# Feed-forward groups 1 and 2: a tile's gate and up products as seven block products in place of eight

## What is computed

```python
def swiglu(x, w_gate, w_up, w_down):
    return (jax.nn.silu(x @ w_gate) * (x @ w_up)) @ w_down

f1 = swiglu(rmsnorm(x, ffn1_pre_g), ffn1_w_gate, ffn1_w_up, ffn1_w_down)
x = x + 0.5 * rmsnorm(f1, ffn1_post_g)
...                                   # the mixer
f2 = swiglu(rmsnorm(x, ffn2_pre_g), ffn2_w_gate, ffn2_w_up, ffn2_w_down)
x = x + 0.5 * rmsnorm(f2, ffn2_post_g)
```

## Time and profile before

| what | value |
|---|---|
| time, three runs | median 1166.08 us (1164.78 to 1174.18) |
| profiled execution, span from first to last instruction | 1167.8 us |
| TensorE busy (matmul) | 1120.6 us, 9522 matmuls |
| VectorE busy | 615.3 us |
| ScalarE busy | 329.2 us |
| GpSimd busy | 42.9 us |
| mean granted TensorE clock | 0.964 |
| DMA | 91.99 MB, mean 79 GB/s |

### The profile page before, as it was taken

The page is one execution under the profiler, slowest core; times in us unless marked ns, Lnnn a source line. Parts: engine busy times, 40 slices in busy tenths (PEclk is TensorE's granted clock), DMA queues, the critical chain, the costliest instruction groups (busy, mean ns, idle before and its releaser), DMA issues. The chain is left out here.

```text
span 1167.8 us, 22671 instructions
## 1 busy us (share of the span) xinstructions
PE 1120.6 (96%) x9522; PEld 1097.9 (94%) x9522; DVE 615.3 (53%) x1015; ACT 329.2 (28%) x496; POOL 42.9 (4%) x57
## 2 busy tenths in 40 slices
PE   6999999999999999999899989999999999999996
PEld 6999999999999999999777789999999999999996
DVE  5534344323434778788869637873434333243446
ACT  5321222112222334331234433442122221122221
POOL 0000000000000000030223000000000000000001
PEclk9999999999999979999779989899999999999998
DMA  6322323222232221232601002213232322222222
GB/s 216 95 80 90 108 72 103 78 90 91 72 108 72 73 86 38 63 88 60 96 2 39 2 1 93 73 41 95 77 113 72 108 72 90 90 82 98 72 73 77
DMA packets 35394, 91.99 MB, mean 79 GB/s; under 512 B 10368, under 2 KB 12928, under 8 KB 35328
## 3 DMA queue, kind: packets, MB, share of 16 engines
q1 hardware_dynamic: 34320, 88.78, 25.0%
q10 hardware_dynamic: 1008, 2.27, 0.6%
HBM read 87.76 MB, written 3.28 MB: 78 GB/s over the span
## 5 line engine op out<-in xcount | busy, mean ns | idle before, releaser
L306 PE MATMUL ps<-xh,wh 128*128 128x272 f32 x1840 | 404.0, 293 | 16.4 <-DVE xl L503 8.6
L306 PE MATMUL ps<-xh,wl 128*128 128x272 f32 x1840 | 400.3, 291 | 0.0
L306 PE MATMUL ps<-xl,wh 128*128 128x272 f32 x1840 | 399.3, 290 | 0.0
L306 PEld LDWEIGHTS ps<-xh,wh 128*128 128x128 f32 x1840 | 299.3, 191 | 19.0 <-DVE wl L289 9.0
L306 PEld LDWEIGHTS ps<-xl,wh 128*128 128x128 f32 x1840 | 299.6, 191 | 0.0
L306 PEld LDWEIGHTS ps<-xh,wl 128*128 128x128 f32 x1840 | 297.7, 191 | 0.0
L284 ACT ACTIVATE wh<-raw 128x1024 fp32r<-128x1024 f32 (+1 forms) x163 | 168.1, 1034 | 324.6 <-PE ps L306 208.6
L289 DVE TENSOR_TENSOR wl<-raw,wh 128x1024 fp32r<-128x1024 f32 (+1 forms) x163 | 192.8, 1203 | 38.0 <-ACT wh L284 37.7
L306 PE MATMUL ps<-hh,wh 128*128 128x272 f32 x704 | 157.7, 290 | 0.0
L306 PE MATMUL ps<-hh,wl 128*128 128x272 f32 x704 | 156.7, 290 | 0.0
L306 PE MATMUL ps<-hl,wh 128*128 128x272 f32 x704 | 156.5, 289 | 0.0
(11 more groups left out here) (312 smaller groups left out, 790.3 us busy)
## 6 DMA issues: line engine op xcount, KB each, us to landing
raw<-in_w_gu SPq DMA_DIRECT2D x88, 512.0 KB, 3.6
raw<-in_w_d SPq DMA_DIRECT2D x32, 512.0 KB, 3.6
raw<-in_w_in SPq DMA_DIRECT2D x19, 512.0 KB, 3.6
raw<-in_w_d SPq DMA_DIRECT2D x16, 384.0 KB, 3.0
raw<-in_w_out SPq DMA_DIRECT2D x8, 512.0 KB, 3.6
out_y<-x SPq DMA_DIRECT2D x16, 136.0 KB, 1.7
x<-in_x ACTq DMA_DIRECT2D x4, 272.0 KB, 5.6
x<-in_x SPq DMA_DIRECT2D x4, 272.0 KB, 6.7
```

The source lines that it names most:

```text
L306: last = pe.matmul(out[:, n], left[:, s, j], right[:, j, n * H:n * H + H], start=first and opens and j == order[0], stop=final and closes ...
```

## The change

Groups 1 and 2 of both blocks (32 of the 44 hidden tiles) compute gate and up together. The two weight tiles, each halved along the 1024 rows, make a 2 x 2 block matrix (row blocks gate and up, column blocks the halves); the activations, halved along the rows and along the tokens, make another. The 2 x 2 block product, eight block products in the kernel before, is done with seven (Strassen's scheme in Winograd's form), each of 4 x 3 = 12 matmuls: 84 a tile where there were 96.

- **Sums of weights.** Four of the seven left factors are not blocks of the weights but sums of them. GpSimd makes them, four additions of 128 x 512 a tile (`fast_pool`), in columns of `xh` and `xl` that the seven products don't read. All seven factors are then split as before, by five ScalarE copies (`fast_hi`) and five VectorE subtractions (`fast_lo`) a tile, three of 512 and two of 1024 columns, where there were two and two of 1024. The seven factors have one buffer each.
- **Sums of activations.** Four right factors are sums too. They are made once for each feed-forward block, while TensorE does the down units of group 0, in four rounds: ScalarE scales two rows (`rows_act`), GpSimd adds (`ffn_pool`), ScalarE and VectorE split (`rows_hi_act`, `rows_lo_dve`).
- **Recombination.** A tile uses four PSUM banks, alternately 0 to 3 and 4 to 7. The products 0, 2, 4, 6 pile up in one bank, and ScalarE copies what lies there after 0, 2 and 4 (`fast_copy`), so TensorE waits for a copy ahead of the products 2, 4, 5 and 6. VectorE adds the pieces (`fast_first`, `fast_gate`), and multiplies by the norm, and by the up result in two halves (`fast_hidden`).
- **Loads.** A tile's gate and up weights come by one transfer of 1 MB into one of two buffers, issued when VectorE has split the tile but one before. The loads of the group's down units follow, and wait for the last but one tile's split.
- **Around it.** In group 1 and 2 the last weights' splits of the down units are ordered anew beside the tile's work (`fast_act`, `fast_dve`), evictions of the group before move into the gaps of the first tile's five subtractions, and group 2's squares for the norm come three down units later in ScalarE's list. Semaphores of the two blocks are merged.

```diff
+        seven = at("ffn", "seven", [2, 4, 4, H], F32R, offset=TB)
+        raw2 = at("ffn", "raw2", [2, KD, P], offset=TB + 32 * 4 * H)
+        qb = at("ffn", "qb", [2, N], offset=TB + 32 * 4 * H)
+        qq = at("ffn", "qq", [4, H], offset=TB + 32 * 4 * H + 8 * N)
+        sums = (at("ffn", "sums0", [4, N], offset=XH), at("ffn", "sums1", [4, N], offset=XH + KD * 4 * N))
+        five = (at("ffn", "five0", [H], offset=WH + 7 * 16 * P), at("ffn", "five1", [H], offset=WH + 15 * 16 * P))
...
+        def fast_sp(sp, q, g, u):
+            f0, nf = GROUPS[g]
+            with sp.Fori(0, nf // 2) as i:
+                for s in range(2):
+                    sp.wait_ge(S("f_lo"), i * 10 + (5 * (16 * q + f0 - FAST0 + s) + 5))
+                    if s:
+                        sp.wait_ge(S("q_lo"), 4 * q + 4)
+                    else:
+                        sp.wait_ge(S("w_lo"), u + RAW)
+                    src = a[f"w_gu{q}"][bass.ds(i * 4 + (2 * f0 + 2 * s), 2)].rearrange("a p n -> p a n")
+                    sp.dma_start((raw2 if s else raw)[:].rearrange("p a k n -> p a (k n)"), src).then_inc(S(f"f_raw{s}"), 16)
+        def fast_pool(pool, q, g):
+            f0, nf = GROUPS[g]
+            with pool.Fori(0, nf // 2) as i:
+                for s in range(2):
+                    n = 16 * q + f0 - FAST0 + s
+                    gate, up = fast_raw(s, 0), fast_raw(s, 1)
+                    landed(pool, q, g, i, s)
+                    pool.wait_ge(S("f_lo"), i * 10 + (5 * n + 7))
+                    pool.tensor_tensor(sum_(0), up[:, 0:4], up[:, 4:8], ADD).then_inc(S("f_sum"), 1)
+                    pool.wait_ge(S("f_sum"), i * 8 + (16 * q + 16 + 4 * n + 1))
+                    pool.tensor_tensor(sum_(1), sum_(0), gate[:, 0:4], SUB).then_inc(S("f_sum"), 1)
+                    pool.wait_ge(S("f_lo"), i * 10 + (5 * n + 9))
+                    pool.tensor_tensor(sum_(2), gate[:, 0:4], up[:, 0:4], SUB).then_inc(S("f_sum"), 1)
+                    pool.wait_ge(S("f_sum"), i * 8 + (16 * q + 16 + 4 * n + 2))
+                    pool.tensor_tensor(sum_(3), gate[:, 4:8], sum_(1), SUB).then_inc(S("f_sum"), 1)
+        def fast_hi(act, q, g, i, s, k, u=None):
+            n = 16 * q + GROUPS[g][0] - FAST0 + s
+            if k in (1, 3):
+                act.wait_ge(S("f_sum"), i * 8 + (16 * q + 16 + 4 * n + k + 1))
+            else:
+                landed(act, q, g, i, s)
+            act.wait_ge(S("f_done"), i * 14 + (7 * n + (1, 3, 4, 6, 7)[k]))
+            if u is not None:
+                act.wait_ge(S("unit_done"), SPL + u - 4 + (1, 2, 2, 3, 4)[k])
+            act.activation(left_to(wh, k), left_of(s, k), ACT.Copy).then_inc(S("f_hi"), 1)
+        def fast_lo(dve, q, g, i, s, k):
+            n = 16 * q + GROUPS[g][0] - FAST0 + s
+            dve.wait_ge(S("f_hi"), i * 10 + (5 * n + k + 1))
+            dve.tensor_tensor(left_to(wl, k), left_of(s, k), left_to(wh, k).bitcast(F32), SUB).then_inc(S("f_lo"), 1)
+        def fast_pe(pe, q, g, i, s, dn):
+            f0 = GROUPS[g][0]
+            n = 16 * q + f0 - FAST0 + s
+            pe.wait_ge(S("h_mul"), i * 2 + (FT * q + f0 + s + 1))
+            pe.wait_ge(S("d_out"), 20 * q + dn + 2 * s + 2)
+            k1, k2, c1, c2 = slice(0, 4), slice(4, KD), slice(0, H), slice(H, N)
+            rights = ((xh[:, k1, c1], xl[:, k1, c1]), (seven[:, 0, 0], seven[:, 1, 0]), (seven[:, 0, 1], seven[:, 1, 1]),
+                      (xh[:, k2, c1], xl[:, k2, c1]), (seven[:, 0, 2], seven[:, 1, 2]), (xh[:, k2, c2], xl[:, k2, c2]),
+                      (seven[:, 0, 3], seven[:, 1, 3]))
+            for m, (high, low) in enumerate(rights):
+                pe.wait_ge(S("f_lo"), i * 10 + (10 + 5 * n + (1, 2, 2, 3, 4, 4, 5)[m]))
+                if m == 1:
+                    pe.wait_ge(S("q_lo"), 4 * q + 4)
+                if m in (2, 4, 5, 6):
+                    pe.wait_ge(S("f_copy"), i * 8 + (4 * n + {2: 1, 4: 3, 5: 2, 6: 4}[m]))
+                out = fast_bank(s, (0, 1, 0, 2, 0, 1, 0)[m])
+                hi, lo_ = slots(wh, m), slots(wl, m)
+                for j in range(4):
+                    for left, right in ((hi, high), (hi, low), (lo_, high)):
+                        last = pe.matmul(out, left[:, j], right[:, j], start=m in (0, 1, 3) and j == 0 and left is hi and right is high,
+                                         stop=j == 3 and left is lo_, skip_group_check=True)
+                last.then_inc(S("f_done"), 1)
+        def fast_copy(act, q, g, i, s, k):
+            f0 = GROUPS[g][0]
+            n = 16 * q + f0 - FAST0 + s
+            act.wait_ge(S("f_done"), i * 14 + (7 * (n + 1) + (1, 2, 3, 5)[k]))
+            if k == 0:
+                act.wait_ge(S("h_mul"), i * 2 + (FT * q + f0 + s + 1))
+            if k == 3:
+                act.wait_ge(S("h_lo"), i * 2 + (FT * q + f0 + s + 1))
+            to = (silu[:, s % 2, 0:H], five[s % 2][:], silu[:, s % 2, H:N], h32[:, s % 2, H:N])[k]
+            act.activation(to, fast_bank(s, (0, 1, 0, 0)[k]), ACT.Copy).then_inc(S("f_copy"), 1)
+        def fast_first(dve, q, g, i, s):
+            n = 16 * q + GROUPS[g][0] - FAST0 + s
+            dve.wait_ge(S("f_done"), i * 14 + (7 * (n + 1) + 4))
+            dve.wait_ge(S("f_copy"), i * 8 + (4 * n + 1))
+            dve.tensor_tensor(silu[:, s % 2, 0:H], fast_bank(s, 2), silu[:, s % 2, 0:H], ADD).then_inc(S("f_part"), 1)
+        def fast_gate(dve, q, g, i, s):
+            n = 16 * q + GROUPS[g][0] - FAST0 + s
+            dve.wait_ge(S("f_copy"), i * 8 + (4 * n + 4))
+            dve.tensor_tensor(h32[:, s % 2, H:N], h32[:, s % 2, H:N], five[s % 2][:], ADD).then_inc(S("f_part"), 1)
+            dve.wait_ge(S("f_done"), i * 14 + (7 * (n + 1) + 6))
+            dve.tensor_tensor(silu[:, s % 2, H:N], fast_bank(s, 1), silu[:, s % 2, H:N], ADD).then_inc(S("f_part"), 1)
+            dve.wait_ge(S("f_part"), i * 6 + (3 * n + 3))
+            dve.tensor_tensor(silu[:, s % 2], silu[:, s % 2], rb[:], MUL).then_inc(S("gate"), 1)
+        def fast_hidden(dve, q, g, i, s):
+            f0 = GROUPS[g][0]
+            n = 16 * q + f0 - FAST0 + s
+            dve.wait_ge(S("silu"), i * 2 + (FT * q + f0 + s + 1))
+            dve.tensor_tensor(h32[:, s % 2, H:N], silu[:, s % 2, H:N], h32[:, s % 2, H:N], MUL)
+            dve.wait_ge(S("f_done"), i * 14 + (7 * (n + 1) + 7))
+            dve.wait_ge(S("h_lo"), i * 2 + (FT * q + f0 + s + 1))
+            dve.tensor_tensor(h32[:, s % 2, 0:H], silu[:, s % 2, 0:H], fast_bank(s, 0), MUL).then_inc(S("h_mul"), 1)
+            hidden_split_dve(dve, q, i, f0, s)
+        def fast_tile_act(act, q, g, i, s):
+            fast_copy(act, q, g, i, s, 0)
+            fast_hi(act, q, g, i, s + 1, 0)
+            fast_copy(act, q, g, i, s, 1)
+            fast_copy(act, q, g, i, s, 2)
+            fast_hi(act, q, g, i, s + 1, 1)
+            fast_hi(act, q, g, i, s + 1, 2)
+            fast_copy(act, q, g, i, s, 3)
+            fast_hi(act, q, g, i, s + 1, 3)
+            silu_act(act, q, i, GROUPS[g][0], s)
+            fast_hi(act, q, g, i, s + 1, 4)
+        def fast_tile_dve(dve, q, g, i, s):
+            fast_lo(dve, q, g, i, s + 1, 0)
+            fast_lo(dve, q, g, i, s + 1, 1)
+            fast_first(dve, q, g, i, s)
+            fast_lo(dve, q, g, i, s + 1, 2)
+            fast_gate(dve, q, g, i, s)
+            fast_lo(dve, q, g, i, s + 1, 3)
+            fast_hidden(dve, q, g, i, s)
+            fast_lo(dve, q, g, i, s + 1, 4)
...
+        def rows_act(act, q, k):
+            if k == 0:
+                if q:
+                    act.wait_ge(S("out"), 6 * 16)
+                act.wait_ge(S("n_rb"), mark(3, 1, 1) + 1 if q else 1)
+                act.wait_ge(S("n_xl"), 3 * KD + 2 * KD if q else KD)
+            else:
+                act.wait_ge(S("f_sum"), 80 * q + 4 * k)
+            act.activation(qb[:, 0], x[:, k], ACT.Copy, scale=par_(f"g{4 * q}", k))
+            act.activation(qb[:, 1], x[:, 4 + k], ACT.Copy, scale=par_(f"g{4 * q}", 4 + k)).then_inc(S("q_act"), 1)
+        def rows_hi_act(act, q, k):
+            act.wait_ge(S("f_sum"), 80 * q + 4 * k + 4)
+            act.activation(seven[:, 0, :, k], qq[:], ACT.Copy).then_inc(S("q_act"), 1)
+        def rows_lo_dve(dve, q, k):
+            dve.wait_ge(S("q_act"), 8 * q + 2 * k + 2)
+            dve.tensor_tensor(seven[:, 1, :, k], qq[:], seven[:, 0, :, k].bitcast(F32), SUB).then_inc(S("q_lo"), 1)
+        def ffn_pool(pool, q, u0):
+            done = S("f_sum")
+            for k in range(4):
+                pool.wait_ge(S("q_act"), 8 * q + 2 * k + 1)
+                if k:
+                    pool.wait_ge(S("q_lo"), 4 * q + k)
+                b11, b12, b21, b22 = qb[:, 0, 0:H], qb[:, 0, H:N], qb[:, 1, 0:H], qb[:, 1, H:N]
+                pool.tensor_tensor(qq[:, 0], b12, b11, SUB).then_inc(done, 1)
+                pool.tensor_tensor(qq[:, 2], b22, b12, SUB).then_inc(done, 1)
+                pool.wait_ge(done, 80 * q + 4 * k + 1)
```

(100 more changed lines are left out.)

118 lines of the change are left out of this document (73 added, 45 removed).

## The result

The changed kernel takes 1163.79 us (median of 16 runs, 1154.43 to 1168.46), the kernel before in the same rounds 1174.17 us (16 runs, 1164.78 to 1179.81): ratio 0.9914, interval 0.9893 to 0.9935. It is 0.9% faster where 3.0% was forecast, and 1163.8 lies outside the range.

The account below looks back on a forecast made before the run. TensorE's matmuls were taken as the bound before the change, VectorE and GpSimd as nearly full after it. 32 x (12.03 - 10.8) = 39.4 us less 4 saves 35.4: 1167.8 to 1132.4 (median 1131), range 1118 to 1158.

Parts of the forecast that it names:

- The price of a sum: Gate and up tiles: a weight sum takes GpSimd 1.0 us and costs a busy VectorE 0.76 us.
- GpSimd beside VectorE: Gate and up tiles: the two engines shut each other out, giving 10.8 us a tile, bounds 10.5 and 11.4.
- second rival: VectorE and GpSimd set the pace at 11.2 to 11.6 us a tile, all sums colliding: 1143 to 1156 us; chance 0.22.
- The sign named in the prediction: The forecast is wrong if GpSimd's sums take 1.5 us.
- That collisions are a matter of chance: A fifth of VectorE's 8.2 us leaves GpSimd's way free, so 3.2 of 4 sums should collide; 10.8 is as if 3.4.
- TensorE's side: Gate and up tiles: 84 matmuls for 96, 10.52 us a tile, 48.1 us saved at most; added waits taken as nothing.
- VectorE's own list: VectorE's operations in one gate and up tile, without GpSimd's hindrance: 8.6 us busy, taken as 8.2 us.
- Group 0's down units: Activation sums there, four rounds chained through three in-order lists, delay group 1: 2 us a block, bounds 0 and 5.
- Loads: 1 MB of gate and up weights lands in 6.0 us, bounds 4.3 and 7.2; the loop fits, 20 us in 21.
- The rest of the kernel: Other group ends, reordered evictions, squares and splits, and GpSimd's mixer part and last lines: each taken as nothing.
- The slower rival: A sum blocks VectorE longer than was saved, from 0.96 us a sum; 1182 us at 1.05, 1207 at 1.25; chance 0.13.

Follow-up runs that it names:

- e1: Changed kernel with all four GpSimd weight sums of each tile cut to 8 of each 128 columns, full ones once a block: 0.9811 of the kernel before.
- e2: Changed kernel with only the fourth GpSimd weight sum of each tile cut to 8 of each 128 columns: 0.9782 of the kernel before.
- v3: Changed kernel with weight sums made by VectorE and VectorE's activation-sum splits one place earlier in group 0's down units: 1131.43 us, 0.9623 of the kernel before.
- v2: Changed kernel with VectorE's split of each activation-sum round ahead of an eviction, not behind it, in group 0's down units: 0.9776 of the kernel before.
- e3: Changed kernel with the third weight sum of each tile made twice, so GpSimd has five sums a tile: 1.020 of the kernel before.
- x1: Changed kernel with 140 long-met waits (70 instructions) added to TensorE's program at one place of the mixer: 1176.4 us, measured one time.
- x2: Kernel before with 372 long-met waits (186 instructions) added to TensorE's program at the same mixer place: 1197.6 us, measured one time.

## Why the prediction failed

- **The price of a sum**, under *GpSimd beside VectorE*, is the step that failed. It was taken as 1.0 us on GpSimd, 0.76 us of it from VectorE, with 3.4 of four colliding. Runs show 1.16 us of holding, 0.85 to 0.89 us from VectorE (1.09 a tile at the margin), and all four collide. 8.0 + 4 x 0.9 = 11.6 us a tile, not 10.8: above the upper bound of 11.4, and the top of the second rival, whose mechanism it is. The sums cost a tile 3.6 us where the forecast had 2.6; about half of the difference is the price, half that all four collide and not 3.4. Averaged over the 32 tiles, the first of each group being partly ready, a tile took 363.2 / 32 = 11.35 us. The sign named in the prediction, sums of 1.5 us, came true: on GpSimd they took 1.55 to 1.69 us in the mean, turns included. The 0.76 came from operations of 32 partitions, the 1.0 from these and the rates of the earlier trace rows. In the kernel after, GpSimd's operations where nothing held them up took 0.77 us for 128x272 and 1.31 for 128x512: 0.54 us for 240 elements, 2.25 ns an element, where the earlier trace rows gave 1.73 to 1.81.
- **That collisions are a matter of chance** was the wrong picture. A fifth of VectorE's list was expected to leave the way free; but GpSimd's four sums start together when a load has landed and the split of the tile ahead frees their place (at 176.56 us after 5.86 us of waiting for the split, at 187.15 after 4.22 for the load), and that is where VectorE's SBUF operations stand in a row (176.5 to 183 us above).
- **TensorE's side** was right: 9138 matmuls, 10.5 us a tile (672 in 84.0 us in e1, e2 and v3), waits on the bank copy ahead of the third product, and one at group 1's start. So was VectorE's own list (8.2 forecast, 8.0 read off), and that ScalarE passes VectorE's lateness on.
- **Group 0's down units**: 2.3 and 2.4 us more, 2 forecast, by the chain of rounds: the fourth split ends at 125.0 us. v2 takes that away.
- **Loads**: 1 MB lands in 4.9 us, not 6.0, with the bound below at 4.3. VectorE's waits show that the loop of loads didn't set the pace.
- **The rest of the kernel** was taken at nothing, without a reason, and lost 10.6 us in the profile, 8 against the mean of three of before. Of the 29.8 us by which the span exceeds the 1132.4 forecast, the stretches are 17.8 (39.4 forecast, 21.6 come true), this 10.6, the rounds 0.7, the remainder 0.7. So the stretches alone would have left the span near 1150, within the range; it took this loss too to carry it beyond 1158. No rival had it; with it the second rival's 1143 to 1156 would have held the result. The cause of most of it is open.
- **The base** was low by chance: the forecast starts from three runs with a median of 1166.08 us, and sixteen have 1174.17. The forecast's 0.970 of that is 1139, so 8 of the 33 us between forecast and result are the base's.
- **The slower rival** needed 0.96 us a sum from VectorE; 0.85 to 0.89 was close. e3 shows the other side: one more sum, and the kernel is 2.0% slower than before.

## What to carry to other kernels

Before work is handed to an idle GpSimd, ask what VectorE does at that moment: here an addition cost VectorE 0.85 us when GpSimd made it and 0.57 us when VectorE made it itself, so the "free" engine was the dearer one (0.991 against 0.975). Where starts on both engines are tied to the same event, count every collision and not a share by busy time: here all four sums of a tile met VectorE's operations (3.6 us a tile), where such a share gave 3.2 and the forecast had 3.4. And don't read the bound off a busy share: VectorE was busy in 95% of the changed kernel's first stretch and set the pace, and in 92% of v3's, where TensorE ran without a gap. Which engine waits for which tells them apart.

## What the runs showed of the hardware

- GpSimd and VectorE took turns by whole operations where both had SBUF operands alone (after, 176.56 to 183.47 us): the rounding, one SBUF input and one output, waited (0.93 us for 0.44) as the subtraction behind it did (1.62 for 0.72). A product that read PSUM ran its usual 0.43 us at 189.53 us, beside a sum from 189.39 to 190.76; before, one of 128x512 that read PSUM took 0.69 us at 503.16 us, inside GpSimd's operation from 502.62 to 505.42.
- 128x272 matmuls with a weight load each ran at 125.0 ns for 84 us at the full granted clock (1.00) beside 95 GB/s of loads (v3).
- The granted clock differs between programs in a stretch whose code is the same: 0.89, 0.85 and 0.76 in the windows above. Over the span it is 0.964 before and 0.954 in the changed kernel; from 574 to 590 us of before it was 0.50.
- Waits long met, 70 and 186 instructions of them in a row, held TensorE up by 0.10 us an instruction in x1 and x2; the some fourteen waits of each of v3's tiles cost nothing (84.0 us, no gap).
